# Places of buffers in SBUF: activations and the shared region lowest, six weight buffers at the upper end

## What is computed

```python
def first_block(x, ...):
    for i in range(DEPTH):                       # stick-breaking, then latent attention
        x = mixers[i % N_MIXERS](x, *layer_params[i])
    return x

def sq_relu_mlp(h, w_up, w_down):
    u = jnp.einsum('btd,df->btf', h, w_up)
    return jnp.einsum('btf,fd->btd', jnp.square(jax.nn.relu(u)), w_down)

def second_block(x, ...):
    for layer in range(DEPTH):
        u = rms_norm_2(h, mix_norm_g[layer])
        h = h + (even_mixer(u, ...) if layer % 2 == 0 else diff_mixer(u, ...))
        h = h + sq_relu_mlp(rms_norm_2(h, mlp_norm_g[layer]), mlp_w_up[layer], mlp_w_down[layer])
    return rms_norm_2(h, final_norm_g)
```

## Time and profile before

| | us |
|---|---|
| median of 3 runs | 1863.65 |
| lowest, highest | 1862.19, 1863.84 |
| the profiled execution, its span | 1862.0 |

### The profile page before, as it was taken

The page is one execution under the profiler, slowest core; times in us unless marked ns, Lnnn a source line. Parts: engine busy times, 40 slices in busy tenths (PEclk is TensorE's granted clock), DMA queues, the critical chain, the costliest instruction groups (busy, mean ns, idle before and its releaser), DMA issues.

```text
span 1862.0 us, 24637 instructions
## 1 busy us (share of the span) xinstructions
PE 1821.1 (98%) x9668; PEld 1442.8 (77%) x9668; DVE 981.3 (53%) x1581; ACT 797.6 (43%) x1401; POOL 478.5 (26%) x475
## 2 busy tenths in 40 slices
PE   7999999999999999999999999999999999999998
PEld 6987777766678766777888888887888788888886
DVE  5355555575546688844443433365677653333433
ACT  5236664455435365564442323233445444241412
POOL 0035551101312145550220201005777112020200
PEclk9999999999999999999999999999999999999999
DMA  5221112231012321012222323222222122323222
GB/s 177 96 71 55 46 46 67 80 92 45 23 57 95 123 72 37 21 33 80 91 97 96 102 91 101 92 91 81 85 81 73 58 93 99 102 91 99 94 93 77
DMA packets 44514, 149.10 MB, mean 80 GB/s; under 512 B 6000, under 2 KB 6384, under 8 KB 44400
## 3 DMA queue, kind: packets, MB, share of 16 engines
q1 hardware_dynamic: 44400, 147.53, 24.5%
HBM read 139.64 MB, written 2.10 MB: 76 GB/s over the span
## 4 chain that ended last, share of the span: by engine, by line
PE 86%; DVE 6%; ACT 3%; POOL 2%; issue 2%; DMA 0%; POOLq 0%; SPq 0%; DVEq 0%; ACTq 0%
PE BANK L286 23%; PE BANK L288 22%; PE BANK L287 22%; PE BANK L918 2%; PE BANK L652 2%; PE BANK L1702 1%; PE BANK L1683 1%; PE BANK L1659 1%; PE BANK L2497 1%; PE BANK L975 1%; PE BANK L637 1%; PE BANK L2472 1%; DVE LH L761 1%; POOL LH L883 1%; DVE WL L263 1%
## 5 line engine op out<-in xcount | busy, mean ns | idle before, releaser
L254 ACT ACTIVATE WH<-WRAW 128x1024 fp32r<-128x1024 f32 x262 | 273.4, 1045 | 465.3 <-PE BANK L288 438.3
L263 DVE TENSOR_TENSOR WL<-WRAW,WH 128x1024 fp32r<-128x1024 f32 (+1 forms) x249 | 325.9, 1310 | 253.7 <-ACT WH L254 252.8
L286 PE MATMUL BANK<-HH,WH 128*128 128x512 f32 x1048 | 423.1, 404 | 12.3 <-DVE WL L263 9.6
L288 PE MATMUL BANK<-HL,WH 128*128 128x512 f32 x1048 | 409.9, 391 | 0.0
L287 PE MATMUL BANK<-HH,WL 128*128 128x512 f32 x1048 | 409.4, 391 | 0.0
L286 PEld LDWEIGHTS BANK<-HH,WH 128*128 128x128 f32 x1048 | 197.7, 189 | 61.8 <-issue 21.8
L288 PEld LDWEIGHTS BANK<-HL,WH 128*128 128x128 f32 x1048 | 197.4, 188 | 42.3
L287 PEld LDWEIGHTS BANK<-HH,WL 128*128 128x128 f32 x1048 | 197.9, 189 | 40.9 <-issue 2.9
L2337 POOL TENSOR_TENSOR HID<-TMP,HID 128x512 fp32r<-128x512 f32 x64 | 83.1, 1299 | 532.4 <-ACT HID L2318 532.4
L286 PE MATMUL BANK<-HID,WH 128*128 128x512 f32 (+1 forms) x520 | 203.8, 392 | 0.0
L288 PE MATMUL BANK<-HID,WH 128*128 128x512 f32 (+1 forms) x520 | 203.6, 392 | 0.0
(11 more groups left out here) (413 smaller groups left out, 3121.5 us busy)
## 6 DMA issues: line engine op xcount, KB each, us to landing
WRAW<-in_w SPq DMA_DIRECT2D x77, 512.0 KB, 3.4
WRAW<-in_wu SPq DMA_DIRECT2D x64, 512.0 KB, 3.3
WRAW<-in_wd SPq DMA_DIRECT2D x64, 512.0 KB, 3.3
WRAW<-in_w0o SPq DMA_DIRECT2D x8, 512.0 KB, 3.5
WRAW<-in_w1o SPq DMA_DIRECT2D x8, 512.0 KB, 3.5
WRAW<-in_wc SPq DMA_DIRECT2D x8, 512.0 KB, 3.3
WRAW<-in_w2o SPq DMA_DIRECT2D x8, 512.0 KB, 3.3
WRAW<-in_w3o SPq DMA_DIRECT2D x8, 512.0 KB, 3.2
```

The source lines that it names most:

```text
L254: e.activation(WH[b % NS][:, 0:n], WRAW[b % NR][:, 0:n], ACT.Copy).then_inc(*inc("s_high", ("high", b)))
L263: e.tensor_tensor(WL[b % NS][:, 0:n], WRAW[b % NR][:, 0:n], WH[b % NS][:, 0:n].bitcast(F32), ALU.subtract).then_inc(*inc("s_low_pool" if p ...
L286: e.matmul(dst, ah, bh, start=first and i == 0, stop=False)
L288: made = e.matmul(dst, ah, bl, start=False, stop=last and i == len(sets) - 1)
```

## The change

The buffers are asked for in another order. HH and HL come first, then the region that the layers share (all the `alias` lists, and MORE within it), then one buffer of 21568 float32, SHARED, that nothing uses and that holds the region's bytes from what follows; then X, WRAW and the small ones; WH and WL last. The reserve for descriptors is set to 1024 bytes. No buffer changes its size.

The instructions of all five engines stand in the same order in both kernels, with the same waits: only the addresses in them differ. The places in the built programs, in bytes of a partition, from first to behind the last:

| buffers | before | after |
|---|---|---|
| reserve | 0 to 16384 | 0 to 1024 |
| X | 16512 to 32896 | 124288 to 140672 |
| HH, HL | 32896 to 65664 | 1152 to 33920 |
| WRAW0, WRAW1 | 65664 to 73856 | 140672 to 148864 |
| WH0 to WH2 | 73856 to 86144 | 189440 to 201728 |
| WL0 to WL2 | 86144 to 98432 | 201728 to 214016 |
| SCR, ST, CF, CB and others | 98432 to 139008 | 148864 to 189440 |
| OG0H, OG0L | 139008 to 171776 | 33920 to 66688 |
| MORE | 139008 to 143104 | 33920 to 38016 |
| region of the layers | 143104 to 229312 | 38016 to 124288 |
| in it: HID0 to HID3 | 143104 to 208640 | 38016 to 103552 |
| in it: OG1H; OG1L | 159488 to 175872; 184064 to 200448 | 54400 to 70784; 78976 to 95360 |
| in it: mqlh, mqll | 208640 to 216832 | 103552 to 111744 |
| in it: mklh, mkll | 220928 to 225024 | 115840 to 119936 |
| in it: ebh, ebl | 191680 to 199744 | 86592 to 94656 |

```diff
-        X = sb("X", [128, KT, T])
         HH = sb("HH", [128, KT, T], FR)
         HL = sb("HL", [128, KT, T], FR)
+        l0g, _, l0v, L0P, LH0, LH1 = alias(
...
+        MORE = sb("MORE", [128, 2 * T])
...
+        og3 = alias([(n, [128, KT, T], FR) for n in ("OG3H", "OG3L")])
+        sb("SHARED", [128, 21568])
+
+        X = sb("X", [128, KT, T])
         WRAW = [sb(f"WRAW{i}", [128, BW]) for i in range(NR)]
-        WH = [sb(f"WH{i}", [128, BW], FR) for i in range(NS)]
-        WL = [sb(f"WL{i}", [128, BW], FR) for i in range(NS)]
         SCR = sb("SCR", [128, 3 * 1280])
...
         TRI = sb("TRI", [128, 256], FR)
-        l0g, _, l0v, L0P, LH0, LH1 = alias(
...
         EPC = SCR[:, 3584:3840]
...
+        WH = [sb(f"WH{i}", [128, BW], FR) for i in range(NS)]
+        WL = [sb(f"WL{i}", [128, BW], FR) for i in range(NS)]
...
-    nc = _bacc.Bacc("TRN2", target_bir_lowering=False, num_devices=1)
+    nc = _bacc.Bacc("TRN2", target_bir_lowering=False, num_devices=1, dynamic_dma_scratch_size=1024)
```

More of the change, by code:

```diff
@@ L142, in alias @@
                 return [c.enter_context(nc.sbuf_tensor(n, s, d)) for n, s, d in specs]
-        X = sb("X", [128, KT, T])
         HH = sb("HH", [128, KT, T], FR)
         HL = sb("HL", [128, KT, T], FR)
-        WRAW = [sb(f"WRAW{i}", [128, BW]) for i in range(NR)]
-        WH = [sb(f"WH{i}", [128, BW], FR) for i in range(NS)]
-        WL = [sb(f"WL{i}", [128, BW], FR) for i in range(NS)]
[L151 to L166, removed]
         l0g, _, l0v, L0P, LH0, LH1 = alias(
@@ L189, in program @@
             ("esc", [128, 1152], F32)])
-        EPC = SCR[:, 3584:3840]
         esum = MORE[0:63, 512:1024].rearrange("p (w n) -> p w n", w=2)
@@ L204, in program @@
         og3 = alias([(n, [128, KT, T], FR) for n in ("OG3H", "OG3L")])
+        sb("SHARED", [128, 21568])
+        X = sb("X", [128, KT, T])
+        WRAW = [sb(f"WRAW{i}", [128, BW]) for i in range(NR)]
+        SCR = sb("SCR", [128, 3 * 1280])
+        ST = sb("ST", [128, 512])
+        CF = sb("CF", [128, 640])
+        CM = sb("CM", [128, 128])
+        CB = sb("CB", [128, 128 * 4], BF16)
+        ROPE = sb("ROPE", [128, 2, T])
+        GC = sb("GC", [128, GAIN_W])
+        RS = sb("RS", [128, T])
+        TMP = sb("TMP", [128, 4, T])
+        EPSC = sb("EPSC", [128, 7])
+        ACC = sb("ACC", [128, T])
+        EHH, EHL = sb("EHH", [128, 2, 62], FR), sb("EHL", [128, 2, 62], FR)
+        RN = sb("RN", [128, NT])
+        RN2 = sb("RN2", [128, NT])
+        QF = sb("QF", [128, 32])
+        TRI = sb("TRI", [128, 256], FR)
+        EPC = SCR[:, 3584:3840]
+        WH = [sb(f"WH{i}", [128, BW], FR) for i in range(NS)]
+        WL = [sb(f"WL{i}", [128, BW], FR) for i in range(NS)]
         eogs = [x[:, i, :] for x, n in ((eog, 6), (eogi, 3), (eogb, 7)) for i in range(n)]
```

## The result

| | us |
|---|---|
| before, median of the 4 runs beside it | 1863.26 (1862.19 to 1863.84) |
| after, median of 4 runs | 1876.95 (1874.96 to 1878.07) |
| ratio, after over before | 1.0074, 95% from 1.0062 to 1.0086 |
| span of the profiled execution, before and after | 1862.0 and 1876.3 |

The kernel became 0.7% slower, 13.7 us by the medians and 14.3 us by the spans. The prediction said 1875.6. The number holds, by luck, and the cause given for it doesn't: it was put down to where the operands lie, low or high, and in the experiments this makes no difference that can be seen. What counts is whether the two operands of a matmul start at the same remainder modulo 256 bytes.

A forecast was written before the change was run, and what follows sets the result against it. TensorE's pace of starting matmuls was taken to bound the kernel, busy 1821.1 of 1862.0 us. Terms of +14.4, -1, -1.5 and 0 gave +11.9 us on the median 1863.65: 1875.6 us, range 1861 to 1884.

The forecast's parts named there:

- the tile at 441.96 us: Latent layer's values, weights moving over mklh and mkll: 232.5 ns, read as the price of moving low, stationary high.
- the same 64%: Chance that both operands must lie low, or the remainders be equal: 1871 to 1884 us.
- a cut at 131072: Byte of the partition below which an operand was counted as low; the cut could lie between 98432 and 138000.
- both theories: Fast matmuls need both operands low in the partition, or both starts at the same remainder modulo 256 bytes.
- HH and HL over the weights: 3144 matmuls of 512 columns, up projections and beside attention, lose both-low places: 226.7 to 232.5 ns, +14.4 us.
- HID, OG and latents: 2224 matmuls of 512 columns with these moving swap sides, 233.3 to 232.5 ns at best: -1.8 to 0, taken -1 us.
- 256 columns: 768 matmuls with weights moving over HH and HL, 120.2 ns, 117 at best after: -2.5 to 0, taken -1.5 us.
- Attention: Small matmuls in four layers' attention, both operands high before, mostly low after: -3 to +3, taken 0 us.
- The signs: Profile after: up projection 216 or 217 matmuls per 50 us, down projection still 216, clock 1.00, waits short.
- If only the moving operand's place counted: Rival, faster: HH and HL over weights lose nothing, the 2224 matmuls fall to 226.7 ns, 1847.5 us; chance 20%.
- the rival of distance: Slower yet: pace grows with distance between the operands; 2 ns more on 5368 matmuls gives 1886 us; chance 3%.
- The rule against which the trace was weighed: Skill page names no dependence on an operand's offset in its partition; by it the change's sum would be nil.

The follow-up runs named there:

- the second experiment: After, with the weights placed low behind HL and pads of 128 bytes before and behind them, so remainders differ by 128: 1875.26 us, 1.0063 of before.
- third experiment: After, with the six weight buffers 128 bytes further up (189568), still high, at the activations' remainder: 1853.26 us, 0.9948 of before.
- the first two experiments: After, with the weights low behind HL: equal remainders, 1849.79 us; then the same with pads shifting the weights by 128 bytes, 1875.26 us.

## Why the prediction was right, and where it was wrong

**The bound.** TensorE's pace, and nothing beside it, set the time: confirmed. PE's busy time grew as the span did, the waits stayed short.

**The cause, wrong.** The step that failed is the reading of two rows: HID at 233.3 ns was put down to its moving operand lying high, and the tile at 441.96 us was put down to its stationary operand lying high. Both also had unequal remainders, and every fast pair of before had equal ones. In before no pair was high with equal remainders or low with unequal ones, so its trace couldn't tell the two apart. The prediction saw this ("if equal remainders are what is fast, every main matmul becomes unequal and the sum is as forecast, by another mechanism") but folded it into the same 64% and gave it no chance of its own. That sentence is what happened. What the runs showed in its place is the remainder: all low, the time is 1849.8 us with equal remainders and 1875.3 with the weights 128 bytes further, and the weights at the upper end are as fast as low ones once they are equal. No run shows a cut at 131072 or anywhere else.

**The sum.** It came out by luck: in this layout both theories make slow what was fast, and leave slow what was slow. In all, +11.9 us were foretold and +13.7 measured. By terms:

1. HH and HL over the weights: +14.4 foretold, +13.3 measured. The settled pitch of after is 232.5 against before's 226.7, as taken. Summed over the pairs, the up projections make 8.7 of it, where 1536 times 5.8 ns is 8.9, and the matmuls beside attention 4.6, where 5.5 were foretold. The prediction has the runs beside attention at 16 to 24 matmuls; in the trace they go from 3 to 144, and 696 matmuls stand in runs of 18 or less.
2. HID, OG and latents: -1 foretold, -0.8 measured. These pairs were unequal before and are unequal after. HID's 0.9 ns, which make the most of it, are no effect of the swap of sides: the second experiment has both levels, 232.4 and 233.3, in one layout.
3. 256 columns: -1.5 foretold, -0.7 measured. The price, 117 ns, came from a tile of another stationary width whose relation of starts was another, too; the row of this case in after is 118.5.
4. Attention: 0 foretold, +1.7 measured with the waits in it, within its bounds.

**The signs.** Foretold were 216 or 217 matmuls in 50 us of HH, 255 or more in 30 us of 256 columns, groups near 395 ns, the clock at 1.00: measured are 217, 256, 395 and 1.00. These held, and none could tell the two theories apart. Of HID it was said that it still holds 216, and it holds 217, which a count of whole matmuls hardly tells apart.

**The rivals.** If only the moving operand's place counted, HID would have risen to 222 and the time fallen to 1847.5: it didn't. By the rival of distance, low activations over weights at the upper end are slow; at equal remainders they are as fast as any pair (third experiment). The rule against which the trace was weighed (the Trainium skill, page "SBUF — State Buffer", section "Who interferes with whom": TensorE has a read port for each operand and never waits on another engine) holds as far as place goes: the kernels with equal remainders, low, high or mixed, lie at 1848 to 1853 us. It says nothing of the two operands' starts, and these are worth 1849.8 against 1875.3 us in the first two experiments.

**What was missed.** A forecast that took the remainder seriously would have seen that the change holds a gain that one pad turns on: the same kernel with 128 bytes more is at 1853.3 us and not at 1876.95, and before itself can be had at 1848.2.

## What to carry to other kernels

Give both operands of the long runs of float32r matmuls (512 columns, 128 by 128 stationary) starts with the same remainder modulo 256 bytes. A pad buffer of 32 floats does it here, and it is worth 0.8% against a kernel in which some six in ten of these matmuls are equal and 1.5% against one with none. Other types and shapes were not tried, and with 256 columns the rule doesn't hold. When two groups of rows differ in pace and in two properties, make the list of all properties that go with it, and find or make the row that separates them before one of them is priced. A forecast can be right to 0.1% on the wrong cause, and then it fails at the next layout.

## What the runs showed of the hardware

- The pitch of float32r matmuls with 512 columns is 226.7 ns when both operands start at the same remainder modulo 256 bytes, else 232 to 234 in most cases and 229 to 231 at three differences (8, 176, 192). With 256 columns equal starts give 119.8 to 120.2 and unequal ones 116.7 to 123.3.
- At equal remainders the pitch is 226.7 ns whether an operand lies low or high in its partition and however far the two are apart: five such kernels took 1849.3 to 1853.3 us. The size of the reserve was never changed alone; HH keeps 226.7 ns with 16384 bytes (before) and with 1024 (before with equal remainders).
- The slow pace of one and the same difference, 128 bytes, is 232.4 ns in one layer and 233.3 in another of the same kernel (second experiment); why is open.
- An unequal stationary operand costs twice, in the matmul under which it is loaded and in its own (232.6 and 234.0 against 226.7 ns). An unequal moving operand cost once, in the one tile that shows it.
